# Start and projection stage of a three-block transformer kernel: load order, the first weight split, and the order of memory and query units

## The reference

```python
cos32, sin32 = rope_tables(positions, A_QK_DIM // ROPE_FRAC)
cos16, sin16 = rope_tables(positions, B_HEAD_DIM // ROPE_FRAC)
mem_n = rmsnorm(mem, g_mem)
h = rmsnorm(x, g_mix[0])                      # x: 512 rows of 1024
mix, q_mem = mixer_a(h, ..., a_w_in, ...)     # h @ a_w_in, split into q, c_kv, k_rope, q_idx, k_idx, w_idx, q_mem
mem_o = memory_cross_attention(q_mem, mem_n, w_mem_kv[0])   # mem_n @ w_mem_kv, for both layers of the network
x = x + concat([mix, mem_o]) @ w_out
```

## Time and profile before

| | |
|---|---|
| runs, us | 2242.83, 2247.15, 2246.04 |
| median, us | 2246.04 |
| profiled execution, us | 2245.39 |
| its span in the trace, us | 2243.6 |
| TensorE busy | 2028.0 us (90%) |
| VectorE busy | 1156.6 us (52%) |
| GpSimd busy | 864.2 us (39%) |
| ScalarE busy | 680.5 us (30%) |
| granted TensorE clock, mean | 0.956 |

### The profile page before, as it was taken

One profiled execution on the slowest core, in us unless ns is written; L12 is line 12 of the kernel. 1 busy time (PEld: TensorE's weight loads), 2 busy tenths in 40 slices (PEclk: granted clock), 3 DMA queues, 4 the chain that ended last, 5 costly groups with the idle time before them and its releaser, 6 DMA issues.

```text
span 2243.6 us, 25866 instructions
## 1 busy us (share of the span) xinstructions
PE 2028.0 (90%) x9596; PEld 1603.1 (71%) x9596; DVE 1156.6 (52%) x2106; ACT 680.5 (30%) x1071; POOL 864.2 (39%) x648
## 2 busy tenths in 40 slices
PE   4989789899999979998999999689998888999996
PEld 3766468687788855566888888567886756888885
DVE  7778873535833867655335433463333466312335
ACT  4242562321122225543222221224444222212211
POOL 4343004345644740124546444132230423444442
PEclk9999999899999988999999999689999999999998
DMA  4222002322622520013225222212120212223221
GB/s 163 82 83 83 13 13 89 139 93 99 223 100 76 215 75 31 25 43 129 94 89 215 100 82 97 85 56 76 57 76 1 94 57 75 88 81 120 97 78 63
DMA packets 32062, 199.14 MB, mean 89 GB/s; under 512 B 3680, under 2 KB 3808, under 8 KB 14048
## 3 DMA queue, kind: packets, MB, share of 16 engines
q1 hardware_dynamic: 27072, 166.74, 21.2%
q10 hardware_dynamic: 4896, 31.15, 3.8%
HBM read 195.78 MB, written 2.10 MB: 88 GB/s over the span
## 4 chain that ended last, share of the span: by engine, by line
PE 49%; DVE 5%; ACT 1%; issue 1%; POOL 1%; DVEq 0%; ACTq 0%
PE psum L1399 43%; PE psum L1421 2%; PE psum L1570 1%; DVE work L960 1%; DVE work L939 1%; PE psum L1535 1%; PE psum L1552 1%; PE psum L1507 1%; PE psum L1806 1%; DVE h_lo L943 1%; DVE work L964 1%; POOL w_lo L555 1%; DVE xT L955 0%; DVE work L949 0%; DVE xT L949 0%
## 5 line engine op out<-in xcount | busy, mean ns | idle before, releaser
L555 POOL TENSOR_TENSOR w_lo<-raw,w_hi 128x512 fp32r<-128x512 f32 (+2 forms) x640 | 856.0, 1366 | 1348.8 <-ACT w_hi L585 1348.8
L1399 PE MATMUL psum<-h_hi,w_hi 128*128 128x512 f32 x1560 | 615.5, 395 | 11.7 <-DVE a_q L992 4.5
L1399 PE MATMUL psum<-h_hi,w_lo 128*128 128x512 f32 x1560 | 612.4, 393 | 0.0
L1399 PE MATMUL psum<-h_lo,w_hi 128*128 128x512 f32 x1560 | 612.2, 392 | 0.0
L585 ACT ACTIVATE w_hi<-raw 128x2048 fp32r<-128x2048 f32 (+2 forms) x176 | 301.4, 1713 | 583.8 <-PE psum L1399 489.1
L1399 PEld LDWEIGHTS psum<-h_hi,w_hi 128*128 128x128 f32 x1560 | 295.0, 189 | 85.1 <-issue 14.7
L1399 PEld LDWEIGHTS psum<-h_hi,w_lo 128*128 128x128 f32 x1560 | 294.5, 189 | 63.7 <-issue 2.4
L1399 PEld LDWEIGHTS psum<-h_lo,w_hi 128*128 128x128 f32 x1560 | 294.7, 189 | 62.5 <-issue 2.3
L1399 PE MATMUL psum<-g_hi,w_hi 128*128 128x512 f32 x528 | 207.0, 392 | 8.5 <-issue 5.0
L1399 PE MATMUL psum<-g_lo,w_hi 128*128 128x512 f32 x528 | 205.5, 389 | 0.0
L1399 PE MATMUL psum<-g_hi,w_lo 128*128 128x512 f32 x528 | 205.5, 389 | 0.0
(11 more groups left out here) (271 smaller groups left out, 2489.4 us busy)
## 6 DMA issues: line engine op xcount, KB each, us to landing
raw<-w_up SPq DMA_DIRECT2D x66, 1024.0 KB, 4.8
raw<-w_dn SPq DMA_DIRECT2D x48, 704.0 KB, 4.0
mod_w<-w_mod ACTq DMA_DIRECT2D x24, 1024.0 KB, 5.0
raw<-w_c_in SPq DMA_DIRECT2D x13, 1024.0 KB, 4.8
raw<-w_b_in SPq DMA_DIRECT2D x7, 1024.0 KB, 4.8
raw<-w_a_idx SPq DMA_DIRECT2D x5, 1024.0 KB, 5.6
raw<-w_a_out SPq DMA_DIRECT2D x8, 640.0 KB, 3.9
raw<-w_b_out SPq DMA_DIRECT2D x8, 640.0 KB, 3.9
```

Of the source, the lines that this page charges most:

```text
L555: ins = nc.gpsimd.tensor_tensor(LO[slot][:, a:z], RAW[slot][:, a:z], HI[slot][:, a:z].bitcast(F32), ALU.subtract)
L1399: ins = nc.tensor.matmul(out, l, r, start=(k == 0 and m == 0), stop=(k == n - 1 and m == 2))
```

## The change

Three things are changed, and two that follow from them.

1. **Loads.** Positions, the five constant columns and the parameters are issued first, from SyncE, ahead of the first unit. The parameters have a semaphore of their own. ScalarE issues none of them.
2. **The start on VectorE and GpSimd.** VectorE writes `w_lo` of the first unit in one instruction of 2048 columns, right behind the first of the four angles, and then all of `h_lo`; the three other angles follow. GpSimd begins with the second unit and no longer adds squares; TensorE sums all eight chunks of squares itself, eight matmuls for two.
3. **Units.** c_kv comes alone, then a unit of queries and a unit of memory by turns four times, then `q_mem`, all in one phase `a_in` of ten units. The slots are: pairs 6 and 7 c_kv, 8 and 9 queries, 10 memory, 11 and 12 queries, 13 memory, 14 and 15 queries, 16 memory, 17 and 18 queries, 19 memory, 20 and 21 `q_mem`. ScalarE's table of the splits (`AFTER_PAIR`) is moved to fit.
4. The high part of the memory moves to another place in SBUF, since it no longer may lie over the squares, and a scratch area for DMAs is made smaller (256).

```diff
-          ("memkv", 4, 2048, [2, 2, 2, 2]), ("a_q", 4, 2048, 2),
+STREAM = [("a_idx", 5, 2048, 2), ("a_in", 10, 2048, 2),
...
+        KINDS = ["ckv"] + ["q", "mem"] * 4 + ["qm"]
...
+            sp.dma_start(POS[:], pos_d.partition_broadcast(P)).then_inc(load_const, 16)
+            sp.dma_start(CST[:, late:NCONST], const_d[:, late:NCONST]).then_inc(load_const, 16)
+            sp.dma_start(PRM[:], params_d).then_inc(load_par, 16)
...
+                pool.wait_ge(lo_ready, 1)
+                for u in range(1, ph.n):
                     low(u // 2, u % 2)
...
-            AFTER_PAIR = {7: 7, 9: 8, 10: 9, 11: 10, 12: 11, 13: 12, 15: 13, 17: 14, 19: 15, 21: 16}
+            AFTER_PAIR = {7: 7, 9: 8, 10: 9, 12: 10, 13: 11, 15: 12, 16: 13, 18: 14, 19: 15, 21: 16}
...
-            v.wait_ge(load_const, 48)
+            v.wait_ge(load_const, 32)
             step(nc.vector.tensor_copy(T[:, 0, :], POS[:]))
             for n, (name, quarter) in enumerate((("32", True), ("32", False), ("16", True), ("16", False))):
-                if n == 2:
+                if n == 1:
+                    v.wait_ge(hi_ready, 1)
+                    nc.vector.tensor_tensor(LO[0][:], RAW[0][:], HI[0][:].bitcast(F32), ALU.subtract).then_inc(lo_ready, 1)
+                    v.wait_ge(load_par, 16)
                     for k in range(DC):
...
-                    pe.wait_ge(x0_added, 3)
-                    for n in range(2):
+                    for n in range(DC):
+                        pe.wait_ge(x0_squared, n // 4 + 1)
```

More of the change, by code:

```diff
@@ L135, in lay_out @@
     w["a_idx"] = units(np.concatenate([misc, qi], 1), 256)
-    w["a_in"] = units(np.concatenate([ckv, q[:, :256]], 1), 256)
-    w["a_q"] = units(np.concatenate([q[:, 256:], qm], 1), 256)
+    q_units = units(q, 256)
+    mixed = [u for pair in zip(q_units, mem_units) for u in pair]
+    w["a_in"] = np.concatenate([units(ckv, 256), np.stack(mixed), units(qm, 256)])
     w["mod"] = x["w_mod_2"][0].T.reshape(24, 2, P, D).transpose(0, 2, 1, 3).reshape(24, P, 2 * D)
@@ L497, in program @@
         EARLY = 6
-        TILES = [("a_in", 0, c) for c in range(2)] + [("a_in", 1, c) for c in range(2)] + \
-            [("memkv", u, c) for u in range(4) for c in range(2)] + [("a_q", u, c) for u in range(4) for c in range(2)]
-        SLOTS = [[0], [1], [2], [3]] + [[4 + 2 * n, 5 + 2 * n] for n in range(4)] + [[12 + n] for n in range(8)]
+        KINDS = ["ckv"] + ["q", "mem"] * 4 + ["qm"]
+        TILES = [(kind, KINDS[:u].count(kind), c) for u, kind in enumerate(KINDS) for c in range(2)]
+        SLOTS = []
+        for i, (kind, u, c) in enumerate(TILES):
+            if kind == "mem" and c == 1:
+                SLOTS[-1].append(i)
+            else:
+                SLOTS.append([i])
+        FREED = []
+        for kind, u, c in TILES:
+            FREED.append(sum(1 for k in FREED if (k[0] == "mem") == (kind == "mem")) + 1)
+            FREED[-1] = (kind, FREED[-1])
         def slot_tiles(p):
@@ L724, in _ @@
             hi_split(2)
+            act.wait_ge(load_const, 32)
             act.wait_ge(x0_summed, 1)
@@ L1262, in _ @@
                 pair_sum(p)
+                ph = PH["a_in"]
                 for i in slot_tiles(p):
[L1264 to L1265 removed]
+                    kind, u, c = TILES[i]
+                    if kind == "mem":
                         continue
[L1267 to L1276 removed]
+                    v.wait_ge(ph.done, i + 1)
+                    if kind != "q":
+                        nc.vector.tensor_tensor((CKV if kind == "ckv" else QM)[:, c, :], bank(i % 2), X0[:],
+                                                ALU.mult).then_inc(ph.free, 1)
+                    else:
+                        rope(bank(i % 2), AQ[:, 2 * u + c, :], C32, S32, 16, ph.free, FREED[i][1], swapped="bank")
                 if p == 6:
@@ L1670, in _ @@
                 last_read[4 + j] = (idx_summed, 2 * len(PAIRS))
-            last_read[7] = (PH["a_q"].free, 6)
+            last_read[7] = (PH["a_in"].free, 10)
             def rank_rest():
@@ L1695, in a_between @@
                     pe.wait_ge(PH["uv"].free, 8)
-            pe.wait_ge(PH["a_q"].free, 8)
+            pe.wait_ge(PH["a_in"].free, 12)
             attend(a_all, a_between)
```

68 lines of the change are left out of this document (24 added, 44 removed).

## The result

| | before | changed |
|---|---|---|
| median of the runs, us | 2244.5 (6 runs beside the changed kernel) | 2251.0 |
| runs, us | 2242.8 to 2247.2 | 2247.2, 2253.8, 2255.5, 2255.6, 2247.8, 2248.2 |
| ratio, 95% interval | | 1.0031 (1.0020 to 1.0043) |
| profiled execution, us (span) | 2245.39 (2243.6) | 2247.19 (2245.4) |
| reciprocal of `x_inverse` starts, us | 50.12 | 39.20 |

The changed kernel is 0.3% slower, 6.5 us on the medians; predicted were 2251.9 us and +5.9. The start gained 10.9 us at the reciprocal, and the slots lost 17.6 us.

A forecast was written before the change was run, and what follows sets the result against it. TensorE is busy for most of the span, so a change is worth what it takes from TensorE's gaps. Start -9.3, slots +11.3 and clock +3.9 make +5.9 us; 2246.04 becomes 2251.9 us, range 2241 to 2259.

The forecast's parts named there:

- The start: VectorE's chain up to the reciprocal: it starts at 40.8 instead of 50.12, a gain of 9.3 us, bounds 5 to 14.5.
- The price of a collision: VectorE's angles beside one `w_lo` of GpSimd: VectorE loses some 3.7 us, and two such pieces fall on three angles.
- The squares on TensorE: Eight matmuls in place of two at the start: 5.6 us more, hidden by VectorE's angles.
- The slots without clock: Pair 10 to pair 21: 95.7 us against 84.4 before, so a cost of 11.3 us (10 to 12.5).
- The clock: Slow TensorE clock behind the three new memory-slot gaps: 1.3 us each, 3.9 us in all (0 to 5.7).
- four waits of 4 us and more: Sign: TensorE would wait for `a_q` this long ahead of second memory tiles.
- The sum: Whole kernel: -9.3 + 11.3 + 3.9 = +5.9 us, giving 2251.9 us.
- The stage ends earlier or later as a whole: Behind the changed stage: what follows waits on nothing from before, so the +5.9 us was added to the total time.
- Alternation is free: Rival on the slots: memory slots cost 8.2 us wherever they stand, so 2236.7 us, faster; chance 13%.
- No clock price: Rival on the slots' gaps: they return at 2.4 GHz or the slow stretch falls on waits; 2248.0 us, no change; 12%.
- The start gives all it can: Rival on the start: a gain of 14.5 us, so 2246.7 us, no change; chance 10%.
- The start gives little: Rival on the start: late loads leave the reciprocal at 43 to 45, gain 5 us, 2256.2 us, slower; chance 15%.

The follow-up runs named there:

- pool_squares: start_only, but GpSimd again adds the squares in pairs and TensorE sums two chunks instead of eight; 2242.7 us, ratio 0.9989 to before.
- after_filled: Changed kernel plus 15 unused matmuls of 512 columns ahead of the second memory tile of pairs 13, 16 and 19; 2246.5 us, ratio 1.0008 to before.
- start_only: Kernel before with only parts 1 and 2 of the change (loads and start), units in the old order; 2236.1 us, ratio 0.9964.
- alt_three_late: alt_three with one more wait: GpSimd splits the third unit only after the last angle; 2223.2 us, ratio 0.9909 to before.
- alt_three: Changed kernel with all tiles rotating over three PSUM banks (0, 1 and 6); 2229.2 us, ratio 0.9931 to before.
- start_three: Changed start with the old, grouped order of units, and tiles rotating over banks 0, 1 and 6; 2228.7 us, ratio 0.9928 to before.
- start_three_late: start_three with one more wait: GpSimd splits the third unit only after the last angle; 2226.7 us, ratio 0.9919 to before.
- pool_split: start_only, but GpSimd again writes the first unit's `w_lo` instead of VectorE; 2236.4 us, ratio 0.9954 to before.

## Why the prediction was right, point by point

**The start.** Predicted were 6.0 for VectorE's first instruction, 11.4 for the split, 19.5 for the end of `h_lo`, 14.6 for the first matmul, 40.8 for the reciprocal. Measured: 4.86, 10.21, 17.7, 13.30, 39.20. The small constants took 3.6 us to land, so that VectorE began at 4.86, where I took the middle of arrivals at 4.5 and 8.0; that is 1.1 of the 1.6 us by which the reciprocal came earlier than predicted. The single split took 2.28 (I said 2.4). The three angles took 21.5 (21.3), with both collisions where they were expected. The price of a collision was right (3.7, measured 3.9), but its reading was not: of the three instructions that took 6.05 us before (21.66 to 27.71), only the first half lay beside `w_lo` (18.52 to 24.42); the rest lay beside the adding of squares (24.38 to 32.40). Beside a split alone three take 4.08, and the rest of the 3.9 is in the short instructions (1.41 for 0.43), which the prediction left out. That the two errors cancel is luck. The Trainium skill, "VectorE: DVE Perf Modes", section on the fixed latency of instructions that read SBUF, gave an estimate of 2.3 us for that split by its formula; the trace agrees with 2.28. The squares on TensorE end at 33.65 (26.62 and 7.03 long), ahead of VectorE: hidden, as said. The prediction gave no price to taking the adding from GpSimd; pool_squares shows that it is most of what the start gives (6.6 of 8.4 us in the medians, 5.6 of 8.1 by the ratios), by way of VectorE. What it would give without the earlier loads was not run. The gain at pair 0 is 10.7 (64.36 for 75.06).

**The slots without clock.** 11.2 us, from after_filled, for the predicted 11.3. Slot by slot in that kernel: 11.13 at pair 13 (predicted 11.2), 12.95 at 16 (12.9), 12.34 at 19 (12.4); 7.9 and 6.5, 8.4 and 6.9 between them.

**The clock.** This is the term that was mis-sized: 6.5 for the predicted 3.9, outside my bounds of 0 to 5.7. The step was "the tile and the scores are nearly 4 on TensorE; a slow stretch of that length at 1.2 GHz loses 1.9 of it. I take 1.3 each". In the trace 1.2 GHz lasted over the whole second tile in two of three slots: 5.5 us for 3.1, and a loss of 2.6 and 2.4 with the scores. In the third the clock came back within the tile (4.6 us), and the loss was 1.4. What I held for the most, 1.9, came from 4 us as the length of the slow stretch, but those 4 us were the work at full clock; done at 1.2 GHz the same work lasts nearly twice as long, and the low level lasted with it. I also wrote four waits of 4 us and more; they were 1.48, 3.33, 4.64 and 3.67. The one at pair 10 could not be that long, since I had left that slot as it was, with 1.51 us. In the other three the first tile also starts late (by 0.71, 0.78 and 1.58 us, again for `a_q`); the two waits together are 4.0, 5.4 and 5.3, near the 4.4, 5.4 and 5.7 predicted, and the distances hold. The Trainium skill, "TensorE: Matmul & The Clock Gate", section on HAM oscillation, describes a loop that pays the low clock in each round; here all three new gaps paid, and with fillers none did.

**The sum.** -10.9 + 17.6 = +6.7 at pair 21 (233.67 - 226.75 = 6.92). The medians say +6.5. Start and clock were both larger than I said, by 1.6 and 2.6 us, and partly cancel. That the total comes within 1 us of +5.9 is thus partly luck, and for a second reason: "The stage ends earlier or later as a whole" is not what the trace shows. In the profiled execution only 1.8 of the 6.9 reach the end. The rest was given back between 240 and 1020 us, where the two programs are the same: the shift is 6.4 us at 383, 4.9 at 698, 1.9 at 1020. There the granted clock differs: added up over stretches of 2 us, the share of the clock that was not granted comes to 33 us in before and 23 us in the changed kernel between 240 and 1020, and to 57 and 56 us behind 1020, where the shift stays. The table shows the same in other kernels: the shift against before at P23 and at the end of the span is -9.1 and -12.0 for start_only, +0.5 and +2.3 for after_filled, -20.4 and -17.3 for alt_three_late. So what the rest of the program adds lies between -5.1 and +3.1 us. The changed kernel's own runs fall into 2247.2 to 2248.2 and 2253.8 to 2255.6, with mean granted clocks of 0.956 and 0.952 to 0.953, and the median of 2251.0 lies between the two groups, where there is no run. All this fits a different share of TensorE's gaps that are followed by the low clock. Why a gap is followed by it in one execution and not in another stays open.

**The rivals.** "Alternation is free" fails with two banks and holds with a bank more (alt_three and start_three). "No clock price" is refuted by after_filled. "The start gives all it can" (14.5) and "The start gives little" (5) lie on both sides of 10.9. Of the two conditions of the first, the small constants did land early and the third unit's `w_lo` did meet the angles; with that taken away too, in alt_three_late, the reciprocal comes 14.7 us earlier than before (35.38).

## What to carry to other kernels

A tile that waits for a buffer pays for all that its reader does first: before moving tiles, write down which bank each one needs, who frees it and what that engine has queued ahead. One more bank was worth 7 us to the grouped order and 22 to the alternating one, and with it the order no longer mattered. Where VectorE and GpSimd both work from SBUF, their work should be laid out so that they take turns: an earlier start of the one can be lost if it meets the other. A new gap of TensorE ahead of work on the critical path should be priced at its own length plus a slow tile behind it (1.4 to 2.6 us each here).

## What the runs showed of the hardware

- Where both worked from SBUF, VectorE went at GpSimd's pace per instruction. A short instruction (0.43 us alone) took 1.4 us beside a `w_lo` whose four instructions take 1.49 each (5.97 in all). Eight instructions on `h_lo` took 5.38 alone, 11.11 beside one split and a part of the next, 15.87 beside a split and the adding of squares. The reciprocal kept its 3.34 us beside a split (in alt_three_late it starts at 35.38, the split at 35.55). The rotations, whose instructions have an input in PSUM, took their 0.7 us each beside the split at 60.80 in before. The Trainium skill, "SBUF — State Buffer", section on who interferes with whom, calls this an exclusive lock held for the whole instruction; these numbers agree, with GpSimd's share also stretched (5.0 us for the split at 60.80, 5.3 to 6.8 where VectorE works from SBUF beside it).
- Small loads at the head of a queue: 256 KB landed 3.3 us and 2.5 KB 3.6 us after their issue from SyncE, ahead of the first unit. Issued by ScalarE, while SyncE issued the first unit and x, they took 8.9 and 6.8.
- The low clock behind a gap varies from kernel to kernel at the same place, and the length of the gap alone does not say whether it comes. Behind a gap of 2.39 us ahead of an early pair the next tile took 7.36 us in start_only (65.02 to 72.38), and in the changed kernel, with 2.41 us at the same place, it took 5.73: pair 8 came at 116.09 and at 114.44. At this place it was slow behind 1.60 us (start_three_late), 2.16 (pool_split), 2.39 (start_only) and 2.40 (alt_three), and not behind 2.39 (after_filled), 2.40 (start_three) and 2.41 (changed, alt_three_late).
